# A two-layer decoder trunk on one core: layer border worked tile by tile with its norm steps on VectorE, and a sixth slot for split weights

## The reference, cut to what matters

```python
def _rmsnorm(x, g):
    return x * rsqrt(mean(x * x, axis=-1) + NORM_EPS) * g

def _layer(x, ...):
    mod = silu(c) @ w_ada + b_ada
    sh1, sc1, gt1, sh2, sc2, gt2 = split(mod, 6)

    h = _rmsnorm(x, g_pre_mix) * (1 + sc1) + sh1
    proj = h @ w_in                       # 1024 x 7240: heads, gates, indexer
    mixed = sigmoid(ga) * _moba_attention(...) + sigmoid(gb) * _dsa_attention(...)
    x = x + gt1 * _rmsnorm(mixed @ w_out, g_post_mix)

    h = _rmsnorm(x, g_pre_ffn) * (1 + sc2) + sh2
    f = (silu(h @ w_gate) * (h @ w_up)) @ w_down          # 2816 wide
    return x + gt2 * _rmsnorm(f, g_post_ffn)
```

## Time and profile before

| | us |
|---|---|
| median of three runs | 891.76 |
| range of the three | 891.47 to 892.01 |
| the profiled execution | 891.98 |
| its span, first to last instruction | 890.1 |

### The profile page before, as it was taken

The page is one execution under the profiler, slowest core; times in us unless marked ns, Lnnn a source line. Parts: engine busy times, 40 slices in busy tenths (PEclk is TensorE's granted clock), DMA queues, the critical chain, the costliest instruction groups (busy, mean ns, idle before and its releaser), DMA issues.

```text
span 890.1 us, 11600 instructions
## 1 busy us (share of the span) xinstructions
PE 867.8 (97%) x4241; PEld 713.6 (80%) x4241; DVE 660.2 (74%) x1090; ACT 411.6 (46%) x607; POOL 133.0 (15%) x164
## 2 busy tenths in 40 slices
PE   7999999999999999999999999999999999999996
PEld 5787788888877788888878778888888788888885
DVE  3778999887878767667568899988787865654842
ACT  1264654655636354344336555555564534434421
POOL 6500300200312030110232030020031200000302
PEclk9999999999999999999999999999999999999998
DMA  9787665567442977676634756566744274564611
GB/s 333 298 300 299 214 243 207 216 237 256 143 166 72 361 276 292 246 289 251 235 142 146 292 223 237 214 236 237 244 158 166 73 302 170 219 260 182 209 52 47
DMA packets 35577, 194.61 MB, mean 219 GB/s; under 512 B 4544, under 2 KB 4544, under 8 KB 19008
## 3 DMA queue, kind: packets, MB, share of 16 engines
q1 hardware_dynamic: 33984, 189.62, 57.8%
q0 software_dynamic: 1536, 4.24, 1.5%
HBM read 192.80 MB, written 1.05 MB: 218 GB/s over the span
## 4 chain that ended last, share of the span: by engine, by line
PE 80%; issue 9%; DVE 8%; DMA 2%; POOL 1%; ACT 1%; SPq 0%; DVEq 0%; POOLq 0%; ACTq 0%
PE ps L1142 23%; PE ps L1144 23%; PE ps L1143 23%; PE ps L1196 4%; PE ps L1248 1%; PE ps L1296 1%; DMA raw<-w_ada 1%; DVE pj L983 1%; DVE ffn_m L848 1%; PE ps L1276 1%; DVE x L1006 1%; DVE pj L968 1%; PE ps L1269 1%; PE ps L1268 1%; PE ps L1247 1%
## 5 line engine op out<-in xcount | busy, mean ns | idle before, releaser
L803 DVE TENSOR_TENSOR w_lo<-raw,w_hi 128x2048 fp32r<-128x2048 f32 (+1 forms) x132 | 302.2, 2298 | 52.2 <-ACT w_hi L581 50.3
L1142 PE MATMUL ps<-w_hi,t_hi 128*128 128x512 f32 (+2 forms) x832 | 325.3, 391 | 2.3 <-DVE t_lo L951 1.6
L1144 PE MATMUL ps<-w_hi,t_lo 128*128 128x512 f32 (+2 forms) x832 | 318.7, 383 | 0.0
L1143 PE MATMUL ps<-w_lo,t_hi 128*128 128x512 f32 (+2 forms) x832 | 318.1, 382 | 0.0
L581 ACT ACTIVATE w_hi<-raw 128x2048 fp32r<-128x2048 f32 (+1 forms) x132 | 249.8, 1896 | 25.4 <-DMA raw<-w_stream 16.0
L1142 PEld LDWEIGHTS ps<-w_hi,t_hi 128*128 128x128 f32 x832 | 156.3, 188 | 35.1 <-DVE t_lo L951 3.1
L1144 PEld LDWEIGHTS ps<-w_hi,t_lo 128*128 128x128 f32 x832 | 156.3, 188 | 30.9
L1143 PEld LDWEIGHTS ps<-w_lo,t_hi 128*128 128x128 f32 x832 | 156.5, 188 | 28.6
L1142 PE MATMUL ps<-w_hi,m_hi 128*128 128x512 f32 x240 | 99.6, 415 | 0.3
L1144 PE MATMUL ps<-w_hi,m_lo 128*128 128x512 f32 x240 | 94.3, 393 | 0.0
L1143 PE MATMUL ps<-w_lo,m_hi 128*128 128x512 f32 x240 | 93.7, 390 | 0.0
(11 more groups left out here) (170 smaller groups left out, 898.6 us busy)
## 6 DMA issues: line engine op xcount, KB each, us to landing
raw<-w_stream SPq DMA_DIRECT2D x128, 1024.0 KB, 5.9
ada<-w_ada SPq DMA_DIRECT2D x84, 512.0 KB, 5.0
raw<-w_ada SPq DMA_DIRECT2D x6, 512.0 KB, 11.8
raw<-w_stream SPq DMA_DIRECT2D x4, 656.0 KB, 8.6
scale_t<-gains POOLq DMA_DIRECT2D x4, 512.0 KB, 4.4
gate_t<-gains POOLq DMA_DIRECT2D x4, 512.0 KB, 5.1
pj<-w_ada SPq DMA_DIRECT2D x3, 512.0 KB, 16.1
mixed<-w_ada SPq DMA_DIRECT2D x2, 512.0 KB, 12.5
```

The lines of the kernel that those rows point to most:

```text
L803: nc.vector.tensor_tensor(w_lo[:, U % RING, 0:n], raw[:, U % RAW, 0:n], w_hi[:, U % RING, 0:n].bitcast(F32), ALU.subtract).then_inc(s_lo, 1)
L1142: nc.tensor.matmul(dst, hi, w_h, start=first, stop=False)
L1143: nc.tensor.matmul(dst, hi, w_l, start=False, stop=False)
L1144: return nc.tensor.matmul(dst, lo, w_h, start=False, stop=last)
```

## The change

It has four parts.

1. **Last FFN block and layer border by tiles.** TensorE runs the whole last block of tile 0 (up, down of block 9 with `turn_m` in its middle, down of block 10) before that of tile 1. ScalarE and VectorE get a written-out `last_block` each, in which the border work of tile 0 is put between the FFN work of tile 1. FFN_FILL goes from 23 to 4. In layer 1 chunk 2 of tile 0 is projected ahead of chunk 0 of tile 1, and `turn_h` of tile 1 stands ahead of the last product of that chunk. Step 2 of layer 1 has then only chunk 2 of tile 1 and `turn_index`, and the first index logits move into the projection of chunk 3.
2. **Norm steps.** `inverse_rms` of y moves from GpSimd to VectorE at the layer border and the end for both tiles, and in the middle of a layer for tile 0. On VectorE its six Newton steps become SCALAR_TENSOR_TENSOR in place of TENSOR_SCALAR. Squares of y and the gate's product are done by halves of 512 columns, and TensorE signals each half.
3. **RING from 5 to 6.** Every split is of one unit further ahead. In layer 0 the splits ahead of the first pieces are of three units (3, 4, 5) where they were of two. At the layer border units 2 and 3 are split in `last_block`, 4 and 5 among tile 1's border steps.
4. **Memory.** The room for the sixth slot comes from the scratch of the dynamic transfers (2048 bytes of a partition) and from the place of `ang`. Tile 1's `hbuf` lies in the third buffer of `pj`, and the squares' unused output in `mixed`.

```diff
-RAW, RING = 3, 5
+RAW, RING = 3, 6
-MIXER_FILL, FFN_FILL, TURN_FILL = 16, 23, 4
+MIXER_FILL, FFN_FILL, TURN_FILL = 16, 4, 4
-OWN_NORMS = [n for n, (l, _, of, t) in enumerate(NORMS) if l >= 0 and of == "x"]
+OWN_NORMS = [n for n, (l, mid, of, t) in enumerate(NORMS)
+             if l >= 0 and (of == "x" or t == 0 or not mid)]
...
             for step in range(NEWTON):
-                link(engine.tensor_scalar(e, y, u, y, ALU.mult, ALU.mult))
-                ins = engine.tensor_scalar(y, e, 1.5, y, ALU.subtract, ALU.mult)
+                if engine is nc.vector:
+                    link(engine.scalar_tensor_tensor(out=e, in0=y, scalar=u, in1=y, op0=ALU.mult, op1=ALU.mult))
+                    ins = engine.scalar_tensor_tensor(out=y, in0=e, scalar=1.5, in1=y, op0=ALU.subtract, op1=ALU.mult)
...
+            def last_block(l):
+
+                j, more = N_FF - 1, l + 1 < DEPTH
+                ahead, behind = up_splits(j)
+                split_lo(l, ahead[0])
+                gate_up(l, j, 0)
+                m_lo_split(l, j, 0)
+                gated(l, False, 0)
+                own_rstd(l, False, "y", 0)
+                added(l, False, 0)
...
+                    scaled(0)
+                gate_up(l, j, 1)
+                if more:
+                    own_rstd(l, False, "x", 0)
+                m_lo_split(l, j, 1)
+                if more:
+                    dve.wait_ge(s_shift, 2 * l + 2)
+                    normed(l, False, 0)
+                    split_lo(l, behind[0])
+                    h_lo(l + 1, "h1", 0)
+                    split_lo(l, behind[1])
+                gated(l, False, 1)
+                own_rstd(l, False, "y", 1)
+                added(l, False, 1)
                 if more:
                     scaled(1)
-                    normed(l, mid, 1)
-                    h_lo(to, kind, 1)
+                    split_lo(l + 1, RING - 2)
+                    own_rstd(l, False, "x", 1)
+                    normed(l, False, 1)
+                    split_lo(l + 1, RING - 1)
+                    h_lo(l + 1, "h1", 1)
...
+            for u in range(RAW, RING):
+                split_lo(0, u)
             for l in range(DEPTH):
-                for u in range(RAW, RING):
-                    split_lo(l, u)
                 add_pieces(sum(MIX_PIECES[1]))
...
-                project(l, 1, 0, lambda: turn_h(l, "h1", 1))
+                if l:
+                    project(l, 1, 0)
+                    project(l, 2, 0, lambda: turn_h(l, "h1", 1), KT - 2)
+                else:
+                    project(l, 1, 0, lambda: turn_h(l, "h1", 1))
...
-                down_chunk(l, N_FF - 1, 0)
-                for j in (N_FF - 2, N_FF - 1):
-                    down_chunk(l, j, 1)
+                for t in range(TT):
+                    up(l, N_FF - 1, t)
+                    down_chunk(l, N_FF - 2, t, lambda: turn_m(l, N_FF - 1, t))
+                    down_chunk(l, N_FF - 1, t)
...
-    nc = bacc.Bacc("TRN2", target_bir_lowering=False, num_devices=1)
+    nc = bacc.Bacc("TRN2", target_bir_lowering=False, num_devices=1, dynamic_dma_scratch_size=2048)
```

More of the change, by code:

```diff
@@ L418, in _ @@
             for l in range(DEPTH):
-                for u in range(RAW, RING):
+                for u in range(RING - 2 if l else RAW, RING):
                     load_unit(l, u)
@@ L565, in _ @@
                     finish_shift(n + 5, 2 * l + 2)
-                for i in range(6 + 8 * l, min(10 + 8 * l, len(NORMS))):
-                    norm(i)
         @block.scalar
@@ L721, in _, with silu @@
             h_hi(0, "h1", 1)
+            def silu(l, j, t):
+                n = l * N_FF + j
+                act.wait_ge(s_up, 2 * n + t + 1)
+                if n:
+                    act.wait_ge(s_m, 2 * n + t - 1)
+                nc.scalar.activation(ffn_s[:, t, :], ps[:, QKT + t, 0:256], ACT.Silu).then_inc(s_silu, 1)
+            def last_block(l):
+                j, more = N_FF - 1, l + 1 < DEPTH
+                ahead, behind = up_splits(j)
+                split_hi(l, ahead[0])
+                silu(l, j, 0)
+                m_hi_split(l, j, 0)
+                sum_squares(NORMS.index((l, False, "y", 0)))
+                split_hi(l, behind[0])
+                if more:
+                    sum_squares(NORMS.index((l, False, "x", 0)))
+                silu(l, j, 1)
+                m_hi_split(l, j, 1)
+                split_hi(l, behind[1])
+                if more:
+                    h_hi(l + 1, "h1", 0)
+                sum_squares(NORMS.index((l, False, "y", 1)))
+                if more:
+                    split_hi(l + 1, RING - 2)
+                    split_hi(l + 1, RING - 1)
+                    copy_chunk(l + 1, 0, 0)
+                    sum_squares(NORMS.index((l, False, "x", 1)))
+                    copy_chunk(l + 1, 1, 0)
+                    h_hi(l + 1, "h1", 1)
+                    copy_chunk(l + 1, 2, 0)
+            copy_chunk(0, 0, 0)
+            for u in range(RAW, RING):
+                split_hi(0, u)
+            copy_chunk(0, 1, 0)
             for l in range(DEPTH):
-                copy_chunk(l, 0, 0)
-                for u in range(RAW, RING):
-                    split_hi(l, u)
-                copy_chunk(l, 1, 0)
                 for s in range(2, N_CHUNK + 3):
@@ L758, in _ @@
                         rectify(l, 2 * (s - 3) + 1)
-                    if s < N_CHUNK:
+                    if s < N_CHUNK and (s > 2 or l == 0):
                         copy_chunk(l, s, 0)
-                border(l, True)
-                for j in range(N_FF):
+                middle(l)
+                for j in range(N_FF - 1):
                     ahead, behind = up_splits(j)
@@ L782, in _ @@
                     split_hi(l, behind[1])
-                border(l, False)
+                last_block(l)
         @block.vector
@@ L1010, in _, with middle @@
             made = [0, 0]
-            def border(l, mid):
-                to, kind = (l, "h2") if mid else (l + 1, "h1")
-                more = to < DEPTH
-                gated(l, mid, 0)
-                added(l, mid, 0)
+            def middle(l):
+                gated(l, True, 0)
+                own_rstd(l, True, "y", 0)
+                added(l, True, 0)
+                dve.wait_ge(s_table, 2 + 4 * l + 2)
+                scaled(0)
+                dve.wait_ge(s_shift, 2 * l + 1)
+                own_rstd(l, True, "x", 0)
+                normed(l, True, 0)
+                gated(l, True, 1)
+                h_lo(l, "h2", 0)
+                added(l, True, 1)
+                scaled(1)
+                own_rstd(l, True, "x", 1)
+                normed(l, True, 1)
+                h_lo(l, "h2", 1)
@@ L1171, in project @@
                         ins.then_inc(s_used, 1)
-                    if between and k == KT // 2 - 1:
+                    if between and k == at:
                         between()
@@ L1185, in down @@
                                       first and k == 0, last and k == 1)
+                    if last:
+                        ins.then_inc(s_y, 1)
                     if between and n == 0:
                         between()
-                if last:
-                    ins.then_inc(s_y, 1)
-                elif t == 1:
+                if not last and t == 1:
                     ins.then_inc(s_used, 1)
@@ L1347, in down_chunk @@
                     pe.wait_ge(s_xup, 4 * l + 1 + t)
-                down(l, down_unit(j), t, m_hi[:, j % 2], m_lo[:, j % 2], j == 0, j == N_FF - 1)
+                down(l, down_unit(j), t, m_hi[:, j % 2], m_lo[:, j % 2], j == 0, j == N_FF - 1, between)
             first_modulation()
@@ L1410, in _ @@
                 turn_m(l, 0, 0)
-                for j in range(1, N_FF):
+                for j in range(1, N_FF - 1):
                     up(l, j, 0)
```

166 lines of the change are left out of this document (89 added, 77 removed).

## The result

The changed kernel took 893.08 us (median of 20 runs, 892.04 to 894.96), the kernel before on the same chip 892.01 (20 runs, 891.29 to 893.73). The ratio is 1.0013, interval 1.0007 to 1.0019: slower by 0.1%. The forecast was 890.5, with 887.4 to 893.2 as the range. The time lies in the range, on the other side of the kernel before from where the forecast had it, and 2.6 us above it.

A forecast was written before the change was run, and what follows sets the result against it. TensorE, busy 867.8 of 890.1 us, was taken to bound the kernel. The terms 1.9 - 1.0 - 1.2 - 0.95 = -1.25 took the profiled 891.98 to 890.7, and a median 0.2 lower gave 890.5, range 887.4 to 893.2.

The forecast's parts named there:

- start of layer 0: At `turn_index` of layer 0, a third weight split ahead of the rotation makes TensorE wait: +1.9 us.
- middle, layer 0: Middle of a layer: cheaper roots of x on VectorE let TensorE transpose tile 1's h earlier, -0.5 us in each layer.
- layer border: Border into layer 1: 4.3 us of fills and 1.2 of old waits go, VectorE gives back over half: -2.2 us.
- `turn_qk` of chunk 2: Layer 1: now one projection behind `turn_index`, TensorE waits for splits, a piece and the rotation (8.35 against 7.35): +1.0 us.
- end: End of the kernel: only half of y's squares is left, then half a product and the root: -0.95 us.
- The price of a root: VectorE's inverse root with SCALAR_TENSOR_TENSOR at 0.21 and 0.15 us an instruction: 1.69 us for x, 1.81 for y.
- The rival of the dear roots: The new root form takes what the old took or more (0.27 and 0.27 us): 892.8 us; chance 0.14.
- All four waits: TensorE at the border: 0.45 us for `m_lo`, 1.3 for unit 4, 0.3 at the shift, 1.6 for h's low half.
- The rival in which VectorE keeps up: TensorE doesn't wait at the border or at the new `turn_qk`, so 3.3 us more come: 887.2 us; chance 0.22.
- "Nothing" for the rotation of chunk 4: Waits of 1.4 us in each layer stay: a ring from TensorE's logits through ScalarE and VectorE back makes them.
- The rival of the falling clock: With fewer fills TensorE idles 1.3, 0.3 and 1.6 us inside about 7 at the border, the clock falls: slower; chance 0.09.
- The rival of the late start: Layer 0: units 6 and 7 split ahead of `copy_index` hold back the logits by 2 us too: 892.5 to 894.5; chance 0.11.

The follow-up runs named there:

- one more instruction: The changed kernel plus one GpSimd TENSOR_SCALAR at the very end of that engine's program, behind the last all-reduce: 889.68 us, ratio 0.9975 to the kernel before.
- The run with the fills back: The changed kernel with the trailing GpSimd instruction and FFN_FILL at 23 in place of 4: 894.02 us, ratio 1.0023 to the kernel before.

## Why the forecast was wrong

**The step that failed** is in no term of the sum: the forecast took everything ahead of layer 0 as untouched, so at 0 us. The runs showed 2.6 us there at the first product and 3.4 in the time: GpSimd's stall of 10.8 us ahead of its first TENSOR_SCALAR, which ScalarE's sine and then the norms of the start wait for. The forecast counted the move of the roots from GpSimd to VectorE as a price on VectorE, and asked who waits for GpSimd's roots where they stood. It never asked what the roots did for GpSimd's program as its last instructions. The trace of before has the pair of MODIFY_POOL_CONFIG at L508 with 0.34 us of idle time, so that a change there looked free. It has one sign of a price, at the layer border: GpSimd's first root starts at 455.15, 1.5 us behind the end of the squares that it needs (453.64), and the 7.24 us since GpSimd's copy are put down to "issue". In the middle of a layer the root starts 0.17 us behind its squares (258.04 to 258.21).

```profile
453.45 0.19 ACT L698 ACTIVATION_READ_ACCUMULATOR pj<-ps 128x1 f32 x1
...
446.87 1.04 POOL L478 COPY shift_t<-acc 128x1024 f32<-128x1024 f32 x1
455.15 0.18 POOL L344 TENSOR_SCALAR rms<-ssq 128x1 f32<-128x1 f32 x1 [7.24 <-issue]
```

The other changes to TENSOR_SCALAR in the middle of the program give no price, as they stand in longer idle time of GpSimd, such as the 31.57 us ahead of 269.89 in the changed kernel.

The terms, from the columns "before" and "one more instruction" of the table, where the stall is out of the way:

| Term | forecast | measured | from |
|---|---|---|---|
| start of layer 0 | +1.9 | +1.9 | 63.59 - 61.61, less 0.06 at the first product |
| middle, layer 0 | -0.5 | -0.7 | +1.27 after +1.98 |
| layer border | -2.2 | -2.7 | -1.40 after +1.27 |
| `turn_qk` of chunk 2 | +1.0 | +0.8 | -0.56 after -1.40 |
| middle, layer 1 | -0.5 | -0.6 | -1.20 after -0.56 |
| end | -0.95 | -1.0 | span -2.2, TensorE's end -1.20 |
| sum | -1.25 | -2.2 | span 887.9 - 890.1 (the terms are rounded) |

- *Start of layer 0* was right in size and cause: the wait at `turn_index` (1.75), by itself in the kernel before with six slots as well.
- *The price of a root* was right: 0.22 and 0.16 an instruction for 0.21 and 0.15, a root 1.72 and 1.77 for 1.69 and 1.81. The rival of the dear roots falls.
- *The border* was right as a sum and partly wrong in its reason. All four waits came, each near its size. Two of them stand in no list of waits and show only from start to start, where a matmul of 512 columns has a step of 0.23: 0.46 at the low split of the FFN's last tile, 0.41 at the shift. The other two are 1.32 (471.24 to 472.56, unit 4) and 1.94 (476.57 to 478.51, the low half of h). All are read, like these lines, from the version with the trailing instruction:

```profile
455.90 0.40 PE L1229 MATMUL ps<-w_hi,m_lo 128*128 128x512 f32 x1
456.36 0.50 PE L1227 MATMUL ps<-w_hi,m_hi 128*128 128x512 f32 x1
...
474.54 0.39 PE L1229 MATMUL ps<-w_hi,t_lo 128*128 128x512 f32 x1
474.95 1.32 PE L1279 MATMUL ps<-const,pj 128*128 128x128 f32 x8
```

  Less the step, the four cost 0.23, 1.09, 0.18 and 1.71 for the forecast's 0.45, 1.3, 0.3 and 1.6. That is 3.2 for 3.65, and the 0.4 between them is nearly all of the 0.5 us by which the border is better. The rival in which VectorE keeps up falls with them. But the forecast had VectorE give back over half of the fills' 4.3 us. The run with the fills back shows that the fills are a gain of 4.3 in full, and that what was given back comes from the new order itself, which puts 16 us of VectorE's work between TensorE's two transposes with or without fills.
- *The new wait at chunk 2's rotation* came, as 0.57 us idle and 0.8 in the table. The chain that makes it, ScalarE's split of unit 8 and VectorE's behind it, is the one that was written; its four parts add up to 8.29, not to 8.35.
- *"Nothing" for the rotation of chunk 4* (the fourth one in the forecast's count) was right in number and wrong in reason. The waits of 1.4 us were there before and after, but no ring of logits, exponentials and masks makes them: with the all-reduce out of the rotation's way they are gone from both layers.
- *The clock* stayed full, at 0.998 over the execution, through waits of 0.93 and 1.54 us within 7. The rival of the falling clock falls for the border. The clock did fall ahead of layer 0 in four of the experiments' profiles, to 0.50, a place for which the forecast had no term. No run shows a fallen clock at the border or what it would cost there, so the 0.09 of that rival, which stands in the forecast's sum for "slower", was the author's estimate; the runs showed the full clock in its place.
- *The rival of the late start* falls too: 4.8 us late at `turn_index` and 4.8 at the rotation of chunk 4 (107.71 and 102.94).

With the stall taken out, the change gives 889.68, 0.25% under the kernel before: the forecast's sign, and 2.5 us of gain (2.2 by the spans) where it had 1.25, from a border and middles that gave a little more each.

## What to carry to other kernels

On GpSimd, look at the kind of the last instruction as well as at the first TENSOR_SCALAR: here an all-reduce with its transfer at the end, in place of TENSOR_SCALAR, cost 3.4 us, and moving work off that engine brought it about. One cheap TENSOR_SCALAR behind the last all-reduce paid it back, with its own 11.14 us where nobody waits. And when a short VectorE instruction takes 4 us (here 4.28 in place of 0.22) at the same place in every layer, look at what GpSimd has just begun before explaining it by a chain of waits.

## What the runs showed of the hardware

- GpSimd stood idle for 9.6 to 11.4 us ahead of a TENSOR_SCALAR, with only the pair of MODIFY_POOL_CONFIG (0.006 to 0.037 us each) in between and "issue" as the reason. At the start it did so in the four profiles of programs that end with the all-reduce and its transfer (10.79, 10.50, 10.99, 9.59), and at the end in the six with the trailing instruction, which stands behind them (11.11 to 11.42). At the layer border of the kernel before, behind all-reduce and copy, it was 7.24. That the end of a program decides about its start is in no row of a single trace; it took two kernels to show it.
- In these traces an all-reduce of GpSimd and a VectorE instruction that reads two operands from SBUF shut each other out. All 14 show seven such VectorE instructions each that start within one of the ten all-reduces. Each takes 3.2 to 4.3 us longer than usual, and all go on at the same point, 1.7 to 1.8 us before the all-reduce's recorded end: 4.28 in place of 0.22 for a 128x64 product, 3.59 in place of 0.43 for a 128x256 product, 5.56 in place of 1.28 for a 128x1024 sum. Behind that point others run beside it at their usual time. The other way round, a VectorE split that already runs keeps its usual 2.28 us, and the all-reduce takes 8.06 us in place of 6.11 (7.23 where 1.25 us of a split were left). So one instruction is hit at a time, since those queued behind it come after that point, and the split at 100.03 isn't hit, since it had started. In the kernel before:

```profile
170.04 6.11 POOL L468 PARTITION_ALL_REDUCE acc<-scale_t  x1 [65.54 <-DVE scale_t L822]
171.25 3.59 DVE L918 TENSOR_TENSOR mixed<-mixed,kiT 128x256 f32<-128x256 f32 x1
...
321.25 2.28 DVE L803 TENSOR_TENSOR w_lo<-raw,w_hi 128x2048 fp32r<-128x2048 f32 x1
321.46 8.06 POOL L468 PARTITION_ALL_REDUCE acc<-gate_t  x1 [42.39 <-DVE gate_t L822]
```

  An instruction that has one input in PSUM takes its usual 0.34 us at 170.88, beside the same all-reduce.
- Newton steps on one number a row were cheaper here as SCALAR_TENSOR_TENSOR (0.22 and 0.16 us) than as TENSOR_SCALAR (0.27 and 0.21).
